# Split products with their input buffers at different distances into a kilobyte

## The chip, the cores and the metric

The kernel runs on one core of a Trainium2 chip. The core has a matrix engine (PE, TensorE), a vector engine (DVE, VectorE), an activation engine (ACT, ScalarE), GpSimd (POOL), a sync engine (SP) that here issues the transfers, an on-chip memory of 128 partitions that the engines read from, and an accumulation memory (`ps`, eight banks) that PE writes. The metric is the time of one execution on the device in microseconds, and lower is better.

## The reference, cut to what matters

Two transformer-like blocks are applied to 256 tokens of width 1024, in float32.

```python
# first block
h = rms_norm(x, norm1_g);  proj = h @ w_in            # 1024 x 11296
q, k, v, z, xbc, dt, g_attn, g_ssd = split(proj)
y_attn = moba_attention(norm(q), norm(k), v) @ w_attn_o
y_ssd  = ssd_mixer(z, xbc, dt, ...) @ w_ssd_o
x = x + (sigmoid(g_attn) * y_attn + sigmoid(g_ssd) * y_ssd) @ w_out
x = x + peer_ffn(rms_norm(x, norm2_g), w_peer_q, keys1, keys2, peer_u, peer_v)
# second block: two layers, each with a modulation from c @ ada_w
#   layer 0: neighbourhood attention and a gated recurrence, with 256 context tokens
#   layer 1: gated short convolution; after each a convolutional FFN of width 2816
# peer_ffn: per token and head, the 16 best of 128 x 128 expert pairs;
# act = x . peer_u[expert], out = sum(gelu(act) * gate * peer_v[expert])
```

Nearly all of the arithmetic is products of a weight matrix with the 256 tokens. The tables `peer_u` and `peer_v` have 16,384 rows of 1024, and the kernel multiplies with all of them and masks by the gates.

## The kernel before, in words

A float32 product is made of three matmuls in the type `fp32r`. Each operand is split into a high part and the remainder, and high x high, high x low and low x high are summed in the accumulation memory. This is `product` (lines 373 to 376):

```python
mm(o, w0, x0, ...)            # L374: weights high, input high
mm(o, w0, x1, ...)            # L375: weights high, input low
return mm(o, w1, x0, ...)     # L376: weights low, input high
```

The second argument of `mm` is the weights, a block of 128 x 128 that is loaded into the array (LDWEIGHTS, PEld in the profile). The third is the input, whose 256 columns stream through it. A slice of input is 256 float32, so 1024 bytes in each partition. `first_tiles` (lines 518, 519, 522) and the start of layer 0 (lines 852, 853, 856) write the same three matmuls in another order. In `rows` (lines 460 to 462) the roles are turned round: a block of the input is loaded as weights, and 512 columns of the weight matrix stream.

**The weights** come in units of 128 x 1024 float32 (4096 bytes in a partition). SP fetches each into one of seven slots of `raw`. ScalarE casts it into one of four slots of `wh`, the high part (L1109, `halves`), and VectorE subtracts, which leaves the low part in `wl` in the place of `raw` (L1560, `lows`); in part of the expert stage GpSimd does that (L2290). `wl` and `raw` are one area. PE frees the slots with its last matmul on a unit. A unit has eight blocks of 128 columns, and so 24 matmuls.

**The inputs** are pairs of buffers too. `xah`, `xal` (8 slices) hold the normalised input of most products. `xbh`, `xbl` (16 slices) hold what the output projections of the first block read. `hh` (4 slices) and `arenar0` to `arenar3` (32 slices each) hold the 128 blocks of activations of the experts. `xch`, `xcl` (8 slices) serve the context and the mixed heads in layer 0, `xfh`, `xfl` (22 slices) the FFNs. ScalarE writes the high part of a slice (L1145 and L1149 for `xah`), VectorE the remainder (L1598 and L1602 for `xal`). The rest of the work lies in big arenas `arena1`, `arenap`, `arena2` and `arena3`, cut into views.

**The order** of each engine's work is written out by hand, with semaphores between engines; nothing is planned at run time, and no order depends on an address. **The places** come from the allocator, which puts each tensor behind the last one that is still open on its stack. When a stack closes, the next tensor starts where that stack began. So the areas of the first block, of the expert stage and of the two layers lie over each other. Sizes that matter, in bytes per partition: `wl` 28672, `wh` 16384, `pcol` 2368, `cst` 1024, `modc` 768, `mab` 160, `small` 256, `xah` and `xal` 8192 each. Then come `J1` 2048, `sc1` 9216, `xbh` and `xbl` 16384 each, and `arena1` 99 x 1024.

Of the kernel before, what the change touches and what calls it, by code (L numbers as in the profile page):

```python
# [155 lines left out]
def build(nc, D, out):  # L156
    f32 = mybir.dt.float32
    f32r = mybir.dt.float32r
# [5 lines left out]
    es = ExitStack()  # L164
    with es:
        def sb(stack, name, shape, dt=f32):
            return stack.enter_context(nc.sbuf_tensor(name, shape, dt))
# [5 lines left out]
        m["wh"] = sb(es, "wh", [128, NSPLIT, 1024], f32r)  # L173
        pcol, cst = sb(es, "pcol", [128, NPC]), sb(es, "cst", [128, 2, 128])
        modc, mab, small = sb(es, "modc", [128, 2, 48, 2]), sb(es, "mab", [128, 5, 8]), sb(es, "small", [128, 64])
        xah, xal = sb(es, "xah", [128, 8, 256], f32r), sb(es, "xal", [128, 8, 256], f32r)
        with ExitStack() as part:
            J1, sc1 = sb(part, "J1", [128, 4, 128]), sb(part, "sc1", [128, 9 * 256])
            xbh, xbl = sb(part, "xbh", [128, 16, 256], f32r), sb(part, "xbl", [128, 16, 256], f32r)
            ar1 = sb(part, "arena1", [128, 99 * 256])  # L180
        with ExitStack() as part:
            with ExitStack() as plain_:
                arp = sb(plain_, "arenap", [128, 128 * 256])
            har = [sb(part, f"arenar{i}", [128, 32, 256], f32r) for i in range(4)]
            scp, hh = sb(part, "scp", [128, 8 * 256]), sb(part, "hh", [128, 4, 256], f32r)
        with ExitStack() as part:
            J2, sc2, x2t = sb(part, "J2", [128, 4, 128]), sb(part, "sc2", [128, 9 * 256]), sb(part, "x2", [128, 8, 256])
            with ExitStack() as layer:
                xch, xcl = sb(layer, "xch", [128, 8, 256], f32r), sb(layer, "xcl", [128, 8, 256], f32r)
                ar2 = sb(layer, "arena2", [128, 107 * 256])  # L190
            with ExitStack() as layer:
                xfh, xfl = sb(layer, "xfh", [128, 22, 256], f32r), sb(layer, "xfl", [128, 22, 256], f32r)
                ar3 = sb(layer, "arena3", [128, 64 * 256])
        spill = nc.dram_tensor("x_scratch", (128, 2048), f32, kind="Internal").ap().rearrange("p (a b) -> p a b", b=256)
        ps = [es.enter_context(nc.psum_tensor(f"ps{i}", [128, 512], f32)) for i in range(8)]
# [123 lines left out]
        STEPS, CTX, at = set(), 80, 2  # L319
# [2176 lines left out]
```

## Time and profile before

| | |
|---|---|
| median of 3 runs | 2088.43 us (2088.15 to 2090.45) |
| the profiled execution | 2089.99 us |
| its span, from the first to the last instruction | 2088.2 us, 40,173 instructions |
| matmuls | 16,718, PE busy 2037.9 us |
| VectorE, ScalarE, GpSimd busy | 1548.1, 1119.7 and 280.2 us |
| granted clock of PE, mean | 0.994 |

The duration of a matmul in the profile runs from its start to the modelled end of its last column. Matmuls overlap, so a duration (281 ns for most) is more than the time from one start to the next. The time that one costs is read from the starts, or from how many begin in a stretch.

### The profile page before, as it was taken

The numbers are of one execution on the slowest core, as the hardware profiler recorded it, in microseconds if no ns is written. First come the engines' busy times: TensorE is split into PE (matmuls) and PEld (weight loads), VectorE is DVE, ScalarE is ACT, GpSimd is POOL, SyncE is SP. The second block draws the span as 40 slices with busy tenths as digits, with TensorE's granted clock in tenths as the row PEclk, the third lists the DMA queues.
The fourth block names the chain that finished last, engine by engine and source line by source line (L and its number), as shares of the span: only waits on it lengthen the run. The fifth ranks groups of instructions, "written<-read, shape, count | busy, mean of one in ns | idle before, by whom it ended". The sixth has DMA issues, their size and how long they took to land.

```text
span 2088.2 us, 40173 instructions
## 1 busy us (share of the span) xinstructions
PE 2037.9 (98%) x16718; PEld 1984.0 (95%) x16718; DVE 1548.1 (74%) x2770; ACT 1119.7 (54%) x1742; POOL 280.2 (13%) x265
## 2 busy tenths in 40 slices
PE   7999999999999999999999999999999999999998
PEld 7898998999999999999999999998899998999998
DVE  6887789774999777877876667655567887867764
ACT  5567677545444666554544455555445554445553
POOL 0000000002887644420000000000110000000000
PEclk9999999999999999999999999999999999999999
DMA  5544433667555444446767777533115777655553
GB/s 194 166 152 137 153 121 112 219 205 248 188 184 188 134 142 142 142 152 215 255 236 237 265 244 252 172 108 111 50 54 196 246 250 261 216 186 172 184 181 121
DMA packets 104437, 375.43 MB, mean 180 GB/s; under 512 B 11584, under 2 KB 12224, under 8 KB 103872
## 3 DMA queue, kind: packets, MB, share of 16 engines
q1 hardware_dynamic: 104256, 372.86, 53.4%
q8 instruction: 133, 2.18, 0.4%
q14 instruction: 48, 0.39, 0.1%
HBM read 370.71 MB, written 2.10 MB: 179 GB/s over the span
## 4 chain that ended last, share of the span: by engine, by line
PE 73%; DVE 17%; ACT 5%; DMA 2%; issue 2%; POOL 0%; SPq 0%; POOLq 0%; DVEq 0%; ACTq 0%
PE ps L374 20%; PE ps L375 19%; PE ps L376 19%; DVE wl L1560 3%; PE ps L782 3%; DVE arenap L1918 2%; ACT wh L1109 2%; DVE arena L1713 1%; PE ps L571 1%; PE ps L460 1%; DVE arenap L1883 1%; PE ps L462 1%; PE ps L461 1%; DVE arenap L1878 1%; DMA raw<-in_ada 1%
## 5 line engine op out<-in xcount | busy, mean ns | idle before, releaser
L374 PE MATMUL ps<-xah,wh 128*128 128x256 f32 x2800 | 798.2, 285 | 7.0 <-DVE wl L1560 3.7
L375 PE MATMUL ps<-xal,wh 128*128 128x256 f32 x2800 | 787.0, 281 | 0.0
L376 PE MATMUL ps<-xah,wl 128*128 128x256 f32 x2800 | 786.6, 281 | 0.0
L1560 DVE TENSOR_TENSOR wl<-raw,wh 128x1024 fp32r<-128x1024 f32 (+2 forms) x539 | 637.7, 1204 | 186.5 <-ACT wh L1109 185.1
L1109 ACT ACTIVATE wh<-raw 128x1024 fp32r<-128x1024 f32 (+1 forms) x608 | 620.6, 1036 | 278.3 <-PE ps L376 135.0
L374 PEld LDWEIGHTS ps<-xah,wh 128*128 128x128 f32 x2800 | 527.9, 189 | 21.0 <-issue 9.0
L375 PEld LDWEIGHTS ps<-xal,wh 128*128 128x128 f32 x2800 | 528.2, 189 | 0.5 <-issue 0.2
L376 PEld LDWEIGHTS ps<-xah,wl 128*128 128x128 f32 x2800 | 528.0, 189 | 0.0
L2290 POOL TENSOR_TENSOR wl<-raw,wh 128x1024 fp32r<-128x1024 f32 (+1 forms) x69 | 162.8, 2365 | 1167.4 <-ACT wh L1109 1167.1
L374 PE MATMUL ps<-hh,wh 128*128 128x256 f32 x1024 | 289.9, 283 | 8.2 <-DVE wl L1560 6.5
L375 PE MATMUL ps<-arenar,wh 128*128 128x256 f32 x1024 | 287.7, 281 | 0.0
L376 PE MATMUL ps<-hh,wl 128*128 128x256 f32 x1024 | 287.7, 281 | 0.0
L374 PEld LDWEIGHTS ps<-hh,wh 128*128 128x128 f32 x1024 | 193.0, 188 | 9.6 <-DVE wl L1560 7.7
L375 PEld LDWEIGHTS ps<-arenar,wh 128*128 128x128 f32 x1024 | 193.0, 188 | 0.0
L376 PEld LDWEIGHTS ps<-hh,wl 128*128 128x128 f32 x1024 | 192.9, 188 | 0.0
L2297 POOL TENSOR_SCALAR hh<-cst,scp 128x128 fp32r<-128x128 f32 x192 | 117.3, 629 | 117.1 <-PE ps L782 117.1
L374 PE MATMUL ps<-xfh,wh 128*128 128x256 f32 x416 | 118.2, 284 | 2.4 <-DVE wl L1560 2.4
L376 PE MATMUL ps<-xfh,wl 128*128 128x256 f32 x416 | 117.6, 283 | 0.0
L375 PE MATMUL ps<-xfl,wh 128*128 128x256 f32 x416 | 117.5, 282 | 0.0
L1320 ACT ACTIVATE hh<-arenap 128x256 fp32r<-128x256 f32 x128 | 52.5, 412 | 115.2 <-PE ps L376 115.2
L1656 DVE SCALAR_TENSOR_TENSOR scp<-raw,small,scp 128x512 f32<-128x512 f32 x112 | 80.5, 749 | 28.0 <-DMA raw<-in_ada 26.6
L1958 DVE TENSOR_TENSOR arenar<-arenap,hh 128x256 fp32r<-128x256 f32 x128 | 53.3, 422 | 62.8 <-ACT hh L1320 62.2
(354 smaller groups left out, 3013.6 us busy)
## 6 DMA issues: line engine op xcount, KB each, us to landing
raw<-in_pu SPq DMA_DIRECT2D x128, 512.0 KB, 3.3
raw<-in_pv SPq DMA_DIRECT2D x128, 512.0 KB, 3.7
raw<-in_ada SPq DMA_DIRECT2D x96, 512.0 KB, 4.2
raw<-in_ff_up SPq DMA_DIRECT2D x88, 512.0 KB, 4.2
raw<-in_w_xbc SPq DMA_DIRECT2D x32, 512.0 KB, 3.3
raw<-in_ff_down SPq DMA_DIRECT2D x32, 512.0 KB, 4.0
raw<-in_w_z SPq DMA_DIRECT2D x16, 512.0 KB, 3.2
raw<-in_w_so SPq DMA_DIRECT2D x16, 512.0 KB, 4.2
```

Of the source, the lines that this page charges most:

```text
L374: mm(o, w0, x0, start=start, stop=False, skip_group_check=skip)
L375: mm(o, w0, x1, start=False, stop=False, skip_group_check=skip)
L376: return mm(o, w1, x0, start=False, stop=stop, skip_group_check=skip)
L782: last = mm(P[:, a * 128:a * 128 + 128], o[:, a, :].bitcast(f32), o2[:, a, :], start=True, stop=True)
L1109: put(W.hi(i), W.raw(i), ACT.Copy).then_inc(S["high"], 1)
L1320: put(hh[:, n % 4, :], HA[:, n, :], ACT.Copy).then_inc(S["h_hi"], 1)
L1560: tt_(W.lo(i), W.raw(i), W.hi(i).bitcast(f32), ALU.subtract).then_inc(S["lowV"], 1)
L1656: stt(dst, wv[:, kk, :], by, dst, ALU.mult, ALU.add).then_inc(step[0], 1)
L1918: last = stt(e4[:, :, :, j], p3, float(j), if16[:, tt, s, :, j:j + 1].to_broadcast([128, 8, 16]), ALU.is_equal, ALU.mult)
L1958: tt_(har[n // 32][:, n % 32, :], HA[:, n, :], hh[:, n % 4, :].bitcast(f32), ALU.subtract).then_inc(S["h_lo"], 1)
L2290: nc.gpsimd.tensor_tensor(W.lo(i), W.raw(i), W.hi(i).bitcast(f32), ALU.subtract).then_inc(S["lowG"], 1)
L2297: last = nc.gpsimd.tensor_scalar(ones1[g % 2][:, a, :], iota, lists[:, 0, 4 * g + a:4 * g + a + 1], None, ALU.is_equal)
```

## The change

In front of nine buffers a small tensor is allocated that nothing uses, just so long that the buffer begins at a chosen distance from a multiple of 1024 bytes. `begin` works out the pad from the distance at which the allocator stands, `last_end`, and that starts as 608. The streamed buffers then begin at 0 (`xah`), 64 (`xal`), 160 (`xbh`), 256 (`xbl`), 896 (`hh`), 480 (`xch`), 544 (`xcl`), 192 (`xfh`) and 352 (`xfl`). `arenar0` to `arenar3` follow from what is allocated before them. No instruction is added or removed.

```diff
-        xah, xal = sb(es, "xah", [128, 8, 256], f32r), sb(es, "xal", [128, 8, 256], f32r)
+        def begin(stack, name, at):
+            have = (last_end[0] + 31) // 32 * 32 % 1024
+            room = (at - have) % 1024
+            if room:
+                sb(stack, "before_" + name, [128, room // 4])
+            last_end[0] = at
+        last_end = [608]
+        begin(es, "xah", 0)
+        xah = sb(es, "xah", [128, 8, 256], f32r)
+        begin(es, "xal", 64)
+        xal = sb(es, "xal", [128, 8, 256], f32r)
         with ExitStack() as part:
             J1, sc1 = sb(part, "J1", [128, 4, 128]), sb(part, "sc1", [128, 9 * 256])
-            xbh, xbl = sb(part, "xbh", [128, 16, 256], f32r), sb(part, "xbl", [128, 16, 256], f32r)
+            begin(part, "xbh", 160)
+            xbh = sb(part, "xbh", [128, 16, 256], f32r)
+            begin(part, "xbl", 256)
+            xbl = sb(part, "xbl", [128, 16, 256], f32r)
+            last_end[0] = 64
             ar1 = sb(part, "arena1", [128, 99 * 256])
...
-            scp, hh = sb(part, "scp", [128, 8 * 256]), sb(part, "hh", [128, 4, 256], f32r)
+            scp = sb(part, "scp", [128, 8 * 256])
+            begin(part, "hh", 896)
+            hh = sb(part, "hh", [128, 4, 256], f32r)
+            last_end[0] = 64
...
-                xch, xcl = sb(layer, "xch", [128, 8, 256], f32r), sb(layer, "xcl", [128, 8, 256], f32r)
+                begin(layer, "xch", 480)
+                xch = sb(layer, "xch", [128, 8, 256], f32r)
+                begin(layer, "xcl", 544)
+                xcl = sb(layer, "xcl", [128, 8, 256], f32r)
+                last_end[0] = 64
...
-                xfh, xfl = sb(layer, "xfh", [128, 22, 256], f32r), sb(layer, "xfl", [128, 22, 256], f32r)
+                begin(layer, "xfh", 192)
+                xfh = sb(layer, "xfh", [128, 22, 256], f32r)
+                begin(layer, "xfl", 352)
+                xfl = sb(layer, "xfl", [128, 22, 256], f32r)
```

## Rows read from the trace of the kernel before

**Rows 1.** The page: busy time of the engines, and the chain that ended last.

```profile
PE 2037.9 (98%) x16718; PEld 1984.0 (95%) x16718; DVE 1548.1 (74%) x2770; ACT 1119.7 (54%) x1742; POOL 280.2 (13%) x265
...
PE 73%; DVE 17%; ACT 5%; DMA 2%; issue 2%; POOL 0%; SPq 0%; POOLq 0%; DVEq 0%; ACTq 0%
```

**Rows 2.** Busy time by windows: stretch, length, each engine's busy us (instructions), clock, DMA.

```profile
570.00:620.00 50.00, 50.00 (x425) 50.00 (x424) 47.86 (x144) 22.79 (x27) 43.35 (x18) 1.00 0.57 187
620.00:670.00 50.00, 50.00 (x425) 50.00 (x425) 49.79 (x53) 23.41 (x27) 42.12 (x18) 1.00 0.58 187
1000.00:1050.00 50.00, 50.00 (x426) 50.00 (x426) 38.87 (x56) 22.29 (x34) 0.00 (x0) 1.00 0.69 241
1980.00:2030.00 50.00, 50.00 (x425) 50.00 (x424) 34.06 (x49) 26.73 (x41) 0.00 (x0) 1.00 0.56 171
```

**Rows 3.** Timeline of PE, 600 to 603 us: start, duration, instruction.

```profile
600.18 0.28 PE L374 MATMUL ps<-xah,wh 128*128 128x256 f32 x1
600.30 0.28 PE L375 MATMUL ps<-xal,wh 128*128 128x256 f32 x1
600.41 0.28 PE L376 MATMUL ps<-xah,wl 128*128 128x256 f32 x1
600.53 0.28 PE L374 MATMUL ps<-xah,wh 128*128 128x256 f32 x1
...
600.89 0.28 PE L374 MATMUL ps<-xah,wh 128*128 128x256 f32 x1
...
603.02 0.28 PE L374 MATMUL ps<-xah,wh 128*128 128x256 f32 x1
```

**Rows 4.** Groups by line and form on PE: count, busy us, mean ns, idle before.

```profile
L374 PE MATMUL ps<-xah,wh 128*128 128x256 f32 x2800 | 798.2, 285 | 7.0 <-DVE wl L1560 3.7 <-POOL wl L2290 2.5 <-DVE xal L1843 0.7
...
L374 PE MATMUL ps<-hh,wh 128*128 128x256 f32 x1024 | 289.9, 283 | 8.2 <-DVE wl L1560 6.5 <-DVE arenap L1982 1.7
...
L374 PE MATMUL ps<-xfh,wh 128*128 128x256 f32 x416 | 118.2, 284 | 2.4 <-DVE wl L1560 2.4
...
L782 PE MATMUL ps<-scp,hh 128*128 128x128 f32 x512 | 62.5, 275 | 0.9 <-ACT hh L1305 0.9
L374 PE MATMUL ps<-xbh,wh 128*128 128x256 f32 x192 | 54.4, 283 | 0.7 <-DVE wl L1560 0.7
...
L374 PE MATMUL ps<-xch,wh 128*128 128x256 f32 x160 | 46.3, 289 | 0.6 <-POOL wl L2290 0.6
...
L518 PE MATMUL ps<-xah,wh 128*128 128x256 f32 x120 | 32.1, 295 | 0.4 <-ACT xah L1149 0.4
...
L852 PE MATMUL ps<-xah,wh 128*128 128x256 f32 x24 | 6.0, 281 | 0.0
```

**Rows 5.** Timeline of PE, 1402 to 1404 us.

```profile
1401.63 0.40 PE L460 MATMUL ps<-wh,xah 128*128 128x512 f32 x1
1401.87 0.39 PE L461 MATMUL ps<-wl,xah 128*128 128x512 f32 x1
...
1404.43 0.40 PE L460 MATMUL ps<-wh,xch 128*128 128x512 f32 x1
```

**Rows 6.** Timeline of PE, 905 to 908 us.

```profile
905.73 1.95 PE L782 MATMUL ps<-scp,hh 128*128 128x128 f32 x16
```

**Rows 7.** Instructions that write or read `xah`: count, shortest, median and longest in ns.

```profile
L1145 ACT ACTIVATE xah<-arena x16: 416/417/420, 18.3 to 462.8; 128x256 fp32r<-128x256 f32 x16
L1598 DVE TENSOR_TENSOR xal<-arena,xah x16: 418/422/426, 18.8 to 463.2; 128x256 fp32r<-128x256 f32 x16
```

## What the change was predicted to do

> **What bounds the kernel now.** I read the page first. The matrix engine (PE) is busy 98% of the span, and the chain that ended last lies on it for 73%, nearly all of that on lines 374 to 376, the three matmuls of a split product; VectorE holds 17% of the chain [rows 1]. "Busy" says little of a pipelined engine, so the next view was the one by windows, for the number of matmuls that start in a given time. In three far-apart stretches of 50 us there are 425, 425 and 426 of them [rows 2]: the engine starts them at a fixed beat, and that beat is the limit. The same rows show what the beat does not depend on. In the first, VectorE works 47.9 of 50 us and GpSimd 43.4; in the last, VectorE works 34.1 and GpSimd nothing, and the DMA share moves between 0.57 and 0.69; the clock is 1.00 in all of them, the 2.4 GHz level. Then the timeline gave the beat itself. From the matmul at 600.18 to the one at 603.02 there are 24 steps, so one takes 2.84/24 = 118.3 ns [rows 3]. 256 columns at 2.4 GHz are 106.7 ns; 11.7 ns of each step are something else.
>
> How much hangs on it: lines 374 to 376 run (2800 + 1024 + 416 + 192 + 160) x 3 = 13,776 times, lines 518, 519 and 522 together 360 times, and lines 852 and 853 48 times, with 24 more of line 856 that has the same form [rows 4]. That is 14,208 matmuls x 118.3 ns = 1681 us, 80% of the span. One nanosecond on each is 14.2 us, or 0.7%.
>
> **What the change is, in addresses.** It adds and removes no instruction, no wait and no transfer, and no order is changed. The pads are allocations that nobody writes or reads. Before, the `last_end = [608]` of the diff says where the first buffer began, and as every size up to `arena3` is a whole number of kilobytes, all ten split buffers, the J tables, the scratch and the arenas began at 608 bytes into a kilobyte. `wl` and `wh` lie in front: 28 + 16 kilobytes and 4576 bytes of columns and small tiles come after their start, so they began at 608 - 480 = 128, and they still do. After, the streamed operands begin at 0, 64, 160, 256, 480, 544, 192, 352 and 896, `arenar` at 64 like `xal`, and the arenas at 256, 64, 544 and 352. So the only thing that can move the time is a price that depends on the start address, in three places.
>
> **Place one: the streamed operand of 14,208 matmuls.** Does the 118.3 ns depend on where a stream of one kilobyte starts? Two things in the trace bear on it. First, the weights. Successive blocks of `wh` and `wl` are 512 bytes, so they start in turn at 128 and 640, while the streamed slices start at 608. A block takes three matmuls, 0.35 or 0.36 us in the rows, which round to 0.01 [rows 3]. A price for the distance between weights and stream, counted in a kilobyte, would make blocks alternate by more than that if it were above some 3 ns a matmul; it isn't. Second, the kernel has one kind of product with the roles turned round: lines 460 to 462 stream `wh` and `wl`, 512 columns at a start of 128, against weights from `xah`, `xal` and their like. From 1401.63 to 1404.43 there are 12 steps, 233.3 ns each [rows 5]. Two kilobytes at a start of 128 therefore cost 233.3, one at 608 costs 118.3; the second kilobyte costs 115.0 and a fixed part of 3.3 is left. With a fixed part of 3.3 ns per matmul the kilobyte has one price, 115.0 ns, at both starts. That fixed part isn't measured alone, and this gives the two bounds. If it were nothing, the kilobyte at 128 would cost 233.3/2 = 116.7 and that at 608 118.3, so 608 would be a poor place, and leaving it would be worth up to 1.6 x 14,208 = 24 us. If it were as large as that of a matmul of line 782, the kilobyte at 608 would be the cheap one. Sixteen of these take 1.95 us with the last's 0.275 in it, so (1.95 - 0.275)/15 = 111.7 ns a step, 5.0 above 106.7 [rows 4, 6]. The kilobyte would cost 113.3 at 608 and (233.3 - 5.0)/2 = 114.2 at 128, and leaving 608 would cost up to 0.85 x 14,208 = 12 us. I take 0: the two known starts agree within 1.6 ns under any fixed part in these bounds, and exactly at one well inside them.
>
> The Trainium skill has a rule that speaks against this change (SBUF — State Buffer, Specifications): the memory is read in 16-byte lines, and what costs is crossing to a new one. Old and new starts are all multiples of 32 bytes, so by it each kilobyte has 64 lines wherever it starts, and the sum is 0. No row here shows a start off such a line. It also has one that leaves room for a gain (TensorE: Matmul & The Clock Gate, Back-to-back issue gap): N/2.4 + 2.5 ns, 109.2 for 256 columns, with no word of addresses. The trace disagrees, 118.3 [rows 3]; were the whole difference due to the start, the sum would be an estimated 9.1 x 14,208 = 129 us of gain.
>
> **Place two: ScalarE and VectorE operations** that write or read the moved buffers. The cast to `xah` takes 416 to 420 ns over 16 slices and the remainder in `xal` 418 to 426 [rows 7]; their starts were all 608 and only these spreads are visible. VectorE has 17% of the chain, 355 us [rows 1]; 1% either way on it, as wide as that spread, is 3.6 us. It is a bound for both signs, and I take 0, as a group of operations has one duration over many addresses. ScalarE has 5% of the chain, so the same 1% there is 1 us. In most product stages these engines have room, so the cover is PE itself; it fails in 620 to 670, where VectorE works 49.79 of 50 us in the search for the largest scores [rows 2]. A slower VectorE would be seen there at once; a faster PE would be held up there.
>
> **Place three: transfers.** The DMA target `raw` is unmoved. The transfers into `xT`, J, `xc`, `x2` and `bias` go to moved tiles, but only a few of them and beside other work: 0.
>
> The sum is made against the profiled execution: 2089.99 us (its span is 2088.2), plus 0, is 2090.0. The median of the runs is 2088.43, 1.6 lower, and so is my figure: 2088.4.
>
> **The rivals.**
> *The stall of the streams is a matter of their start, and goes in part.* For it: 6.6 ns of each step are above what the line 782 matmuls need for the same weight load, and nothing in the trace accounts for them. Against it: two starts with the same price per kilobyte. If 608 is a poor place in the sense of the first bound, the gain is 24 us, 2064.7. A stronger form: only a stream that starts at 0 never crosses a kilobyte's edge, and `xah` is now such a one. It is streamed by lines 374, 376, 518, 519, 852 and 853, 5600 + 240 + 48 = 5888 times [rows 4]; down to 111.7 each saves 6.6 ns, 39 us in all, less what the VectorE-bound stretch keeps: 2050 at best.
> *The starts like 128 are the dear ones.* This is the other bound: 0, 64, 256, 192 and 896 are multiples of 64 like 128, while 608 is not. It decides if the fixed part is above 3.3 ns. The price is 0.85 ns a matmul, 12 us, if all the streams pay it: 2100.5. For it: the fixed part of line 782 is 5.0. Against: that figure can be the weight load's own and not the stream's.
> *A different start for the high and the low half costs at each change of stream.* In each three matmuls the stream goes from the high buffer to the low and back. Both began at 608; now they never do. If each change cost as little as 0.4 ns, 2/3 x 14,208 x 0.4 is 3.8 us, 2092.2; at 1 ns it is 9.5 us, 2097.9. No row shows such a change between unequal starts.
> *The change doesn't do what it says.* The pads are computed from the assumed 608; if another figure held, the buffers would be shifted together and the starts would still differ from each other by the same amounts. This changes no number above.
>
> **How the numbers follow.** A measurement of this kernel can tell 0.2%, 4.2 us, from no change. No change has 0.58. The stall going in part has 0.24: 0.15 for a gain of up to 24 us, 0.09 for more. Dear starts have 0.11 and the change of streams, in a size above 4.2 us, 0.07. So faster 0.24, same 0.58, slower 0.18. The range goes from 2070 to 2100: it holds the case of no change, most of the smaller gains (0.11) and most of the slower cases (0.14), 0.83 in all. The likeliest case alone would be 2085 to 2092.
>
> **What would show it.** In the profile after: between 422 and 428 matmuls in each of the stretches of 50 us, and 24 steps in 2.84 us for `xah`; 233.3 ns for the 512-column streams, whose start isn't moved, whatever happens to the rest. If the start matters, the beat will differ between buffers: `xah` with `xal` (0, 64), `hh` with `arenar` (896, 64), `xfh` with `xfl` (192, 352), `xch` with `xcl` (480, 544). One beat of 117.5 or less, or of 119.2 or more, on the first pair alone is enough to make the prediction wrong, as that pair has two thirds of the matmuls. A time that moves with the beat unmoved would mean place two: then the durations of the operations on moved tiles have changed.

## The result, and the profile after

The changed kernel takes 2094.7 us (median of 20 runs, 2088.4 to 2102.6) against 2089.4 us (20 runs, 2084.6 to 2096.0): a ratio of 1.0024, 95% interval 1.0013 to 1.0034. It is slower, by a quarter of a percent. Its runs cover 14.2 us, those of before 11.5 (standard deviations 4.0 and 2.6 us). One run of a kernel further down is left out of its ratio: 2475 us, with a granted clock of 0.75 where the others of that kernel have 0.99. The profiled execution was one of its fastest, 2088.84 us with a span of 2087.1. So the slowdown can't be read off its length; the beat of PE shows it.

First the page of after, the same two lines as in [rows 1].

```profile
PE 2039.2 (98%) x16718; PEld 1986.2 (95%) x16718; DVE 1550.8 (74%) x2770; ACT 1119.5 (54%) x1742; POOL 280.1 (13%) x265
...
PE 74%; DVE 17%; ACT 4%; DMA 2%; issue 2%; POOL 0%; SPq 0%; POOLq 0%; DVEq 0%; ACTq 0%
```

The busy shares moved by nothing that would tell of it. Now the windows of after: stretch, length, busy us (instructions) of PE, PEld, DVE, ACT, POOL, then clock and DMA. Four of them answer to [rows 2].

```profile
570.00:620.00 50.00, 50.00 (x416) 50.00 (x415) 47.82 (x145) 22.41 (x26) 41.48 (x18) 1.00 0.53 184
620.00:670.00 50.00, 50.00 (x416) 50.00 (x415) 49.79 (x49) 21.92 (x25) 42.78 (x18) 1.00 0.54 184
860.00:910.00 50.00, 50.00 (x433) 50.00 (x432) 41.54 (x85) 30.16 (x68) 22.90 (x39) 1.00 0.42 148
1000.00:1050.00 50.00, 50.00 (x428) 50.00 (x427) 39.64 (x57) 22.87 (x32) 0.00 (x0) 1.00 0.68 243
1980.00:2030.00 50.00, 50.00 (x427) 50.00 (x426) 34.08 (x49) 26.91 (x42) 0.00 (x0) 1.00 0.55 179
```

Read the number of matmuls in 50 us. It was 425 in both stretches of the experts' first half; it is 416. It was 426 and is 428 on `hh` and `arenar`, and 425 and 427 in the last FFN. PE is 100% busy each time and the clock is 1.00, so only the count tells. The three matmuls of a product (a step of 355.0 ns before, three times the 118.3 of [rows 3]) now have two beats on `xah` and `xal`. The timeline of after shows both; every third start is a new product:

```profile
640.08 0.28 PE L400 MATMUL ps<-xah,wh 128*128 128x256 f32 x1
...
640.45 0.28 PE L400 MATMUL ps<-xah,wh 128*128 128x256 f32 x1
...
641.53 0.28 PE L400 MATMUL ps<-xah,wh 128*128 128x256 f32 x1
...
1985.07 0.28 PE L400 MATMUL ps<-xah,wh 128*128 128x256 f32 x1
...
1986.13 0.28 PE L400 MATMUL ps<-xah,wh 128*128 128x256 f32 x1
```

Four products take 641.53 - 640.08 = 1.45 us (363 ns each) at 640, and three take 1.06 us (353) at 1985. Taken over all starts of the trace, the pairs behave so, in ns per product:

| pair and starts | before | after |
|---|---|---|
| `xah` 0, `xal` 64 | 355.0 | 353.3, or 363.3, now and then 360.0 |
| `hh` 896, `arenar` 64 | 355.0 | 353.3 |
| `xbh` 160, `xbl` 256 | 355.0 | 353.3 |
| `xfh` 192, `xfl` 352 | 355.0 | 353.3 |
| `xch` 480, `xcl` 544 | 355.0 | 353 to 354 in long stretches, 355 to 357 where eight products stand alone |

In this trace a beat holds from one interruption to the next (a wait of PE, or matmuls of another form), whether that is 14 steps or 454. The two operations shown in [rows 7] kept their durations: the cast to `xah` 417 to 420 ns, the remainder 412 to 425. One part of VectorE's work did get longer, the search for the largest scores; it comes up under the sum below.

### The profile page after: what moved, and what is told of

It is laid out like the page before. It is cut to its first block, busy times and chain, and to the rows that moved or that the text cites. A ratio compares the mean times of both kernels' runs of the same rounds, so it can differ in the third digit from the quotient of the medians.

```text
span 2087.1 us, 40173 instructions
## 1 busy us (share of the span) xinstructions
PE 2039.2 (98%) x16718; PEld 1986.2 (95%) x16718; DVE 1550.8 (74%) x2770; ACT 1119.5 (54%) x1742; POOL 280.1 (13%) x265
## 3 DMA queue, kind: packets, MB, share of 16 engines
q8 instruction: 133, 2.18, 0.4%
## 4 chain that ended last, share of the span: by engine, by line
PE 74%; DVE 17%; ACT 4%; DMA 2%; issue 2%; POOL 0%; SPq 0%; POOLq 0%; DVEq 0%; ACTq 0%
PE ps L400 20%; PE ps L401 20%; PE ps L402 19%; DVE wl L1586 3%; PE ps L808 3%; DVE arenap L1944 2%; ACT wh L1135 1%; DVE arena L1739 1%; DMA raw<-in_ada 1%; PE ps L597 1%; PE ps L486 1%; DVE arenap L1909 1%; PE ps L488 1%; PE ps L487 1%; DVE arenap L1904 1%
## 5 line engine op out<-in xcount | busy, mean ns | idle before, releaser
L1135 ACT ACTIVATE wh<-raw 128x1024 fp32r<-128x1024 f32 (+1 forms) x608 | 620.2, 1036 | 286.1 <-PE ps L402 136.5
```

The source lines that it names most:

```text
L1135: put(W.hi(i), W.raw(i), ACT.Copy).then_inc(S["high"], 1)
```

## The experiments

**Which buffers.** The first two kernels take the change apart.

```diff
 # only_xa: xah at 0, xal at 64, everything else back at 608
+        begin(es, "all", 608)
-            begin(part, "xbh", 160)
+            begin(part, "xbh", 608)      # and so for xbl, hh, xch, xcl, xfh, xfl
 # not_xa: the reverse
-        begin(es, "xah", 0)
+        begin(es, "xah", 608)            # and xal at 608, all others as in the change
```

> Only xah (0) and xal (64) are moved; all other streamed buffers and the arenas stay at 608. Theory (start of the streams): the product of three matmuls on xah and xal takes either 353.3 ns or 363.3 ns, and which one is settled anew after each pause; on all other pairs it takes 355.0 as before. So the slowdown of the change stays and its small gain on the other pairs goes: 1.003 to 1.006 of before. Rival (the arenas and the scratch moved, and VectorE or ScalarE pay): 1.000, and 355.0 everywhere. Rival (the whole shift is noise between programs): within 0.1% of before, with the two beats hidden behind other waits.

Measured: 1.0036 (1.0024 to 1.0048), 2096.0 us. The trace has 355 on the other pairs. On `xah` and `xal`, counted in stretches of six or more, some 1,350 products take 353, 180 take 360 or 361 and 1,020 take 363.

> The reverse: xah and xal stay at 608, and all other pairs and the arenas begin where the change puts them. Theory: 355.0 ns a product on xah and xal, 353.3 on the 1792 products of the other pairs, so 3 us less than before, 0.9985, and little spread between runs. Rival (the arenas and VectorE pay): slower than before by about 0.2%, as the change.

Measured: 0.9991 (0.9982 to 1.0001), 2087.4 us, with 355 on `xah` and `xal` and 353 on nearly all the rest. The interval doesn't tell the 3 us from nothing, but it excludes the slowdown. So the loss comes with one pair, and the new places of the arenas have no visible part in it.

> The change with xah at 896 in place of 0 (xal stays at 64): the pair of starts that hh and arenar have in the change, where every product took 353.3 ns. Theory: 353.3 on all 4736 products, so (4736 x 1.67) 7.9 us less than before, 0.996, with little spread. Rival (it is the number of products or the work beside them on xah and xal that brings the long beat, and not where they start): the long beat of 363.3 stays in the same stages, 1.002.

```diff
-        begin(es, "xah", 0)
+        begin(es, "xah", 896)
```

Measured: 0.9982 (0.9972 to 0.9992), 2086.2 us. The long beat is gone: about 2,500 products on the pair at 352 to 354. It is the starts and not the work beside them. The gain is half of what I expected; the last experiment shows where the rest goes. Little spread, which I had expected twice, didn't come either: the runs cover 12.1 us here and 8.4 with `xah` and `xal` at 608.

**The same program twice.**

> The changed kernel once more, for a second profile. Theory (each stretch of products takes its beat at its start, and not always the same in two executions): another set of stretches on xah and xal shows 363.3, all other pairs again 353.3 throughout, and a product more on the long beat is worth up to 10 ns of span against the first profile. Rival (the program fixes the beats): the same stretches as in the first profile show 363.3, and the span stays within 1 us of 2087.1.

Measured: 2099.07 us, span 2097.3, 10.2 us more than the first profile of the same program. These are the windows of this second execution:

```profile
620.00:670.00 50.00, 50.00 (x415) 50.00 (x414) 49.79 (x49) 22.44 (x26) 42.74 (x18) 1.00 0.51 180
860.00:910.00 50.00, 50.00 (x423) 50.00 (x422) 41.60 (x88) 29.43 (x65) 23.70 (x41) 1.00 0.39 136
1000.00:1050.00 50.00, 50.00 (x428) 50.00 (x427) 39.95 (x58) 24.99 (x35) 0.00 (x0) 1.00 0.72 253
1980.00:2030.00 50.00, 50.00 (x416) 50.00 (x415) 34.84 (x54) 27.30 (x45) 0.00 (x0) 1.00 0.53 175
```

The stretches 860 to 910 and 1980 to 2030 changed from 433 to 423 and from 427 to 416, with 1000 to 1050 the same. Of some 2,550 products of the pair in stretches of six or more, about 945 had the long beat in the first execution and 1,665 in the second: 720 x 10 ns is 7.2 us, and 110 more at 360 make it 8. A stretch at the 1.2 GHz level that only the second trace has (at 1126 us) accounts for another 1.7. The program doesn't fix the beat. That adds to the spread of the changed kernel's runs but isn't all of it: the runs of before cover 11.5 us, and its trace has one beat throughout. The granted clock varies too, from 0.991 to 0.995 in runs of before.

**What the beat depends on.** A program of its own runs only products on one pair of weight buffers and one of streams, at chosen starts, with pauses between:

```python
W0, W1 = (t[:, s // 4 + 128 * q:s // 4 + 128 * q + 128] for t, s in ((wh, w), (wl, u)))
X0, X1 = xh[:, h // 4 + 256 * k:h // 4 + 256 * k + 256], xl[:, l // 4 + 256 * k:l // 4 + 256 * k + 256]
mm(o, W0, X0, ...)
mm(o, W0, X1, ...)
last = mm(o, W1, X0, ...)
```

> A program of its own, which leaves the whole computation out: the three matmuls of a product, sixteen products in a row, after pauses of six kinds, for 28 sets of starts of weights, high stream and low stream. No other engine works beside it but for short ScalarE casts in the pauses. Theory A (the distance between stream and weights, counted in a kilobyte, sets the beat): weights 0 with streams 480 and weights 544 with streams 0 behave as weights 128 with streams 608, 355.0 ns. Theory B (the start of the stream alone): weights 0 or 544 make no difference to streams 0 and 64, which show 353.3 or 363.3. Theory C (the distance between high and low stream): all sets with equal starts give 355.0, and those 64 apart the two beats. If only the work of VectorE and GpSimd beside PE brings the long beat, no set here shows it.

Measured, in ns per product (the times of different pauses, from the starts in the timeline):

| weights | streams high, low | ns | streams minus weights |
|---|---|---|---|
| 128 | 608, 608 | 355 | 480 |
| 0 | 480, 480 | 355 | 480 |
| 544 | 0, 0 | 355 | -544 |
| 32 | 512, 512 | 355 | 480 |
| 128 | 96, 96 | 355 | -32 |
| 128 | 0, 64 | 353, 360 or 363 | -128, -64 |
| 0 | 896, 960 | 353, 360 or 363 | 896, 960 |
| 544 | 416, 480 | 353 or 363 | -128, -64 |
| 128 | 128, 128; 0 and 0, 0 alike | 360 | 0 |
| 128 | 0, 0 | 356 or 360 | -128 |
| 128 | 64, 64 | 340 or 353 | -64 |
| 128 | 160, 160 | 350, once 353 | 32 |

Theory A is right and stronger than I had it: 480, -544 and -32 are the same number modulo 256, and so are -128 and 896. Theory B falls on 0, 0: 360 with weights at 0 and 356 or 360 with weights at 128. Theory C falls on 64, 64, which has two beats with equal starts. No other engine worked beside PE here, so what PE does itself is enough for the effect. That its two reads meet in the memory, the weights for the next matmul and the stream of this one, is the natural reading; no run shows what happens inside.

> The program of its own again, with the whole computation left out: all sets start the weights at 128. First sixteen sets with both streams at the same distance, 0 to 240 bytes in steps of 16, then the 56 sets with two different distances in steps of 32. Theory (each matmul's time depends on the distance of its stream from the weights that are loaded beside it, modulo 256 bytes): the distance 192 (which is 64 in front) gives 353.3 and 340.0 as start 64 did, 224 gives 355.0, 0 gives 360.0, 32 gives 350.0; and a set with distances c and d lies between what c and d give alone. Rival (the period is a kilobyte): the distance 192 behaves otherwise than 64 in front.

Measured, with both streams at one distance, for 0, 16, 32, ... 240 bytes: 360, 350 or 356, 350 (353 once), 355, 353, 355 or 360, 360, **340**, 356 or 360, 356, 352 or 356, 358, **340 or 353**, 350 or 358, 355, 352. The period of 256 holds. With two different distances the sum isn't a mean of the two: all 56 sets lie at 349 to 360 and none is as good as the equal pair at 112. (The fourth program has one set of 112 with 192; it took 347 after some pauses and 356 to 361 after others.)

> The program of its own, with the whole computation left out, for what settles the beat: five sets of starts, fifty stretches each of twelve products, after ten kinds of pause in turn (one to five small float32 matmuls, or a wait for ScalarE of five lengths). Theory A (the kind of pause fixes it): at starts 0 and 64 every fifth of the same kind shows the same beat. Theory B (it is where the pause ends against a slower clock): the same kind shows both. Starts 608 show 355.0 and starts 240 show 340.0 after every kind.

Measured at starts 0 and 64: after two or four of the small matmuls always 353, after one, three or five always 363, after waits for ScalarE both. (The very first stretch was still at the slower clock.) In the timeline of that program, six products after two and six after three small matmuls:

```profile
21.20 0.28 PE L48 MATMUL ps<-xh,wh 128*128 128x256 f32 x1
...
23.32 0.28 PE L48 MATMUL ps<-xh,wh 128*128 128x256 f32 x1
...
26.13 0.28 PE L48 MATMUL ps<-xh,wh 128*128 128x256 f32 x1
...
28.31 0.28 PE L48 MATMUL ps<-xh,wh 128*128 128x256 f32 x1
```

2.12 us against 2.18. So at these starts A holds for pauses of PE's own, and those that another engine ends give both beats; that the reason is the moment at which such a pause ends, as B has it, is not shown. The kind isn't all, though: in the first survey, at the same starts, two small matmuls gave 363 and four gave 360. With both streams at 64 the kind alone decides in this program: 353 after two or four small matmuls, 340 after all others, waits included. Streams at 608 show 355 after every kind. Those at 240 show 340 in the end after every kind, but after some kinds the first two to four products of a stretch take 345 to 358 before it settles.

**Into the kernel.**

> All ten streamed buffers and the arenas begin at 64, so 64 bytes before the weights, the distance at which the survey showed 353.3 ns a product after some pauses and 340.0 after others. Theory (the distance of each stream from the weights sets the beat, and the start of a stretch which of two it is): every product of the kernel shows 353.3 or 340.0, never 360 or more; 4736 products x 1.67 = 8 us less than before if all take the long one, 4736 x 15 = 71 us if all take the short one; 2018 to 2082. Rival (the survey's 340.0 needs idle engines beside PE, or equal content): 353.3 throughout, 2082. Rival (different starts of high and low are what helped hh, xb, xc and xf): 355.0, no change.

```diff
-        begin(es, "xah", 0)
+        begin(es, "xah", 64)             # and all other streamed buffers at 64
```

Measured: 0.9926 (0.9899 to 0.9952), 2072.4 us, 2061.6 to 2079.0. Both beats appear on every pair, 340 to 344 on some 2,040 products and 353 on 2,155, none longer. The theory stands; the rivals don't.

> The same with all at 160, 32 bytes behind the weights, where the survey showed 350.0 ns after nearly all pauses. Theory: 350.0 to 353.3, so 4736 x 5 = 24 us less at best, 2066 to 2082. Rival (only the survey, without other engines, shows it): 355.0, no change.

Measured: 0.9936 (0.9916 to 0.9956), 2076.8 us. Of the products in longer stretches some 3,665 take 350 and 530 take 353 or 354.

> The weights begin 16 bytes later in their slots (144 modulo 256) and all streams at 256, so each stream begins 112 bytes behind the weights modulo 256, the distance at which the second survey showed 340.0 ns a product after every pause. Theory (distance alone): 340.0 on all 4736 products, in every stage; that is 15.0 ns less on each, 71 us if PE is the limit everywhere, and some 10 us of it kept by VectorE where it works 49.8 of 50 us: 2018 to 2032, with a small spread. Rival (with other engines at work the good distance is not stable): two beats again, 2050 to 2075. Rival (a start off 32 bytes costs on VectorE and ScalarE): PE at 340.0 and the time above 2040.

```diff
-        m["wl"] = sb(es, "wl", [128, NRAW, 1024], f32r)
+        m["wl"] = off(sb(es, "wl", [128, NRAW * 1024 + 64], f32r), NRAW)   # starts 16 bytes in
```

Measured: 1.0047 (1.0034 to 1.0061), 2100.2 us: a miss, and slower than anything. The products took 350, 355 or 360. VectorE and ScalarE kept their durations (1204 and 1035 ns for the two splits of a unit, 1204 and 1036 before), so neither rival named the reason. Only 630 or so products came down to 350, and 2,300 took 358 to 361.

> The program of its own, with the whole computation left out, twenty sets of starts in which high and low weights are set apart. Question: why distance 112 gave 350 to 360 in the kernel. If weights off a multiple of 32 are the reason, the set 144, 144, 256, 256 shows 350 or more, and 160, 160, 272, 272 and 0, 0, 112, 112 show 340. If it is that high and low weights were 256 apart (400 and 144), the set 400, 144, 256, 256 alone is long, and 128, 384, 240, 240 too. If neither, both show 340 and the cause is elsewhere in the kernel. Starts 496, 752 and 1008 for the streams show what 240 shows if the period is 256 bytes.

Measured: weights 144 with streams 256 give 360 after every pause. Weights 160 with 272, 128 with 240, 0 with 112 and 256 with 368 settle at 340, after up to four products at 345 to 357. All have a distance of 112. Six products each, at weights 144 and at weights 128:

```profile
34.00 0.28 PE L51 MATMUL ps<-xh,wh 128*128 128x256 f32 x1
...
36.16 0.28 PE L51 MATMUL ps<-xh,wh 128*128 128x256 f32 x1
...
206.77 0.28 PE L51 MATMUL ps<-xh,wh 128*128 128x256 f32 x1
...
208.81 0.28 PE L51 MATMUL ps<-xh,wh 128*128 128x256 f32 x1
```

High and low weights 256 apart changed nothing (128, 384 with 240: 340), nor did streams at 496, 752 or 1008. So a distance keeps the beat that it settles at when both starts move by a multiple of 32 bytes, in all sets tried, but not when they move by 16. That cuts both ways: weights 144 with streams 624 (distance 224) take 360 where 128 with 608 take 355, but weights 144 with streams 80 (distance 192) settled at 340 after every kind of pause, where 128 with 64 has two beats. This explains the products at 360 in the kernel with all at 112. Where its 350 and 355 come from stays open: the program of its own shows only 360 at those starts.

> The weights stay at 128. All streams but hh and arenar begin at 240 modulo 256, so at the very starts that gave 340 to 343 ns in both surveys; hh and arenar begin at 64 as in the run with all at 64. Theory (the distance counts, and starts that are an odd multiple of 16 must be on the side of the stream as in the survey): 340 on all 3712 products of the other pairs, 340 or 353.3 on the 1024 of hh and arenar; 3712 x 15 + 1024 x 1.7 = 57 us less at most, 10 us of it kept by VectorE: 2031 to 2045. Rival (the kernel's weights lie in seven and four slots of 4 kilobytes and the survey's in one, and that is why 112 failed): 350 to 360 again, 2085 to 2102.

```diff
+        def stream(stack, name, n, at):
+            begin(stack, name, at)
+            last_end[0] = at + 32
+            return sb(stack, name, [128, n * 256 + 8], f32r)[:, 4:4 + n * 256].rearrange("p (a b) -> p a b", b=256)
-        xah = sb(es, "xah", [128, 8, 256], f32r)
+        xah = stream(es, "xah", 8, 736)  # begins at 752, 240 modulo 256; xal, xb, xc, xf too
```

Measured: 0.9861 (0.9841 to 0.9882), 2059.8 us, the best of all: 30 us less than before and 35 less than the change. The products settle at 340 on all pairs but `hh` and `arenar`, which show 340 or 353. Many short stretches begin with two or three products at 353, as in the survey, and so average 343. The rival on slots falls. A window of before and four of this kernel, and PE's wait in its view of waits:

```profile
660.00:680.00 20.00, 17.53 (x148) 17.32 (x148) 15.87 (x27) 9.98 (x13) 11.45 (x6) 1.00 0.59 185
...
570.00:620.00 50.00, 50.00 (x443) 50.00 (x443) 47.97 (x139) 23.98 (x28) 45.41 (x20) 1.00 0.59 198
620.00:670.00 50.00, 44.05 (x389) 43.85 (x387) 49.28 (x63) 19.50 (x23) 33.78 (x14) 0.97 0.55 182
660.00:680.00 20.00, 11.01 (x81) 10.81 (x80) 11.91 (x31) 6.95 (x9) 8.45 (x6) 0.74 0.28 94
1920.00:1970.00 50.00, 50.00 (x444) 50.00 (x443) 37.79 (x56) 29.03 (x46) 0.00 (x0) 1.00 0.58 196
...
PE ps L398 <- POOL wl L2314: 9.0, 1, 9.0
```

443 and 444 matmuls in 50 us, where there were 425. The gain was less than the 45 to 57 us forecast. Summed over the steps of the trace, the shorter beats are worth 50 us; the span is 32.5 us shorter. About half of the difference goes in the stretch in the middle. VectorE works 49.28 of 50 us, PE gets ahead of it and then waits, once, for 9.0 us (2.5 in the kernel before); its clock fell to 1.2 GHz for 10.2 us. Against the kernel before, the same matmul came 11.6 us earlier at 660 and 4.7 us earlier at 680. The rest goes in smaller pieces elsewhere; the whole trace has 42.9 us at the 1.2 GHz level, the one of before 27.5. `xah` at 896 lost its gain in the same place: 2.6 us ahead before the stretch, 2.1 behind after it, with 6.8 us at 1.2 GHz. (That is the trace of its slowest run, 2090.2 us; its median is 2086.2.)

## Why the prediction was wrong

**The step that failed** is place one, "I take 0". PE's beat does depend on where a stream starts: on the first pair it went from 118.3 ns a matmul to 117.8 or 121.1, past the 119.2 that I had named as a sign of being wrong. It depends on the distance from the weights modulo 256, and I had two arguments against that, both blind to it. The measured time, 2094.7 us, lies inside the range from 2070 to 2100 all the same, but that is luck: none of the causes that the range was drawn for brought it there.
- *Successive weight blocks at 128 and 640 would alternate, were there a price for the distance.* They are 512 bytes apart, two whole periods. An even beat excluded a period of a kilobyte, not one of 256 bytes.
- *Two starts, 608 and 128, have one price per kilobyte.* With the roles turned the distance is 128 - 608 = -480, so 32 modulo 256; in the products it is 224. The comparison was of two distances that are close in price (350 and 355 a product in the surveys) and said nothing of the other fourteen. My bounds, 0.85 to 1.6 ns a matmul, were bounds for those two starts. The measured span over all distances is 340 to 363 a product, so 5 ns a matmul to the good and 2.8 to the bad.

**The sum with the measured beats.** The first execution of the change has, against 355.0, about 1,550 products of the pair at -1.7 ns, 950 at +8.3 and 70 at +5, and 1,792 of the other pairs at -1.7: +2.7 us. The second has +10.6. Measured in the spans are -1.1 and +9.1. Two more things lie between. One is the slow clock: the trace of before has 27.5 us at the 1.2 GHz level, these two have 23.5 and 24.7, which at half speed is worth 2.0 and 1.4 us. The other is the long stretch of 455 products from 513 to 679. It costs PE 3.8 us in both sums, but the chain lies on VectorE there, and PE waits at its end anyway. What counts is how long VectorE's search takes, from its cast to its last reduction (start and duration, before and then after; the times in ns are shortest, median and longest):

```profile
L1896 DVE CAST arenap<-arenap x1: 1168/1168/1168, 565.5 to 565.5; 128x512 f32<-128x512 uint32 x1
L1922 DVE TENSOR_REDUCE arenap<-arenap x4: 2286/2286/2290, 630.0 to 672.3; 128x128 f32<-128x2048 f32 x4
...
L1922 DVE CAST arenap<-arenap x1: 2297/2297/2297, 564.5 to 564.5; 128x512 f32<-128x512 uint32 x1
L1948 DVE TENSOR_REDUCE arenap<-arenap x4: 2285/2286/2287, 631.2 to 674.4; 128x128 f32<-128x2048 f32 x4
```

That is 109.1 us before and 112.3 after, with the same operations: 3.2 us more, and they are VectorE's. The times are 112.2 in the second execution and in only_xa, which have the 363 beat in this stretch too, and 109.0 in not_xa. So they go with `xah` and `xal` and not with the new places of the arenas. The operations that got longer ran while GpSimd worked: of the 16 additions in L1899, the eight with no GpSimd operation beside them take 404 to 415 ns in all these traces, and the eight with one take 651 to 707 in before and not_xa and 718 to 831 in the other three. Why they fall differently beside GpSimd is not shown; other kernels here have 108.5 to 111.8. With these terms the sums are +0.1 and +8.6 us, against -1.1 and +9.1. The median of 20 runs lies between, at +5.3.

**The rivals.** Dear starts had the right sign and 11%, but another mechanism: it made all multiples of 64 dear, and `hh`, `arenar` and `xfh` at such starts became quicker. A price for each change between high and low doesn't exist as such (160 and 256 are quicker than two equal starts at 608). The stall going in part was right for four of the five pairs: 1.7 ns a product. The pair with nearly two thirds of the products went the other way in part of its stretches.

**What stood.** Place three. Place two stood for the casts and remainders of the streams, and not_xa has the moved arenas without a loss, but it had missed that VectorE's search can change its length, by 3.2 us, with no address of its own involved. The figure of 0.7% per nanosecond is an upper bound: in the last kernel 5 ns on about three quarters of the matmuls would be 56 us, of which it kept 30. The note that a faster PE would be held up at 620 to 670 came true. The sentence on 512-column streams was wrong: their start didn't move, but the start of their weights (`xah`, `xch`) did, and their mean step fell from 233.2 to 232.3 ns (231 to 233 by stretch, where all were 233).

**The Trainium skill's rules.** The runs show starts that are all multiples of 32 at 340, 350, 353, 355 and 363 ns, so the number of 16-byte lines, by which I would have had 0 (Trainium skill, SBUF — State Buffer, Specifications), isn't what decides. The Trainium skill says too that PE has two independent read ports and that loading the next weights "doesn't steal SBUF read bandwidth from the running matmul" (TensorE: Matmul & The Clock Gate, Step-by-step: what each phase is for). The surveys speak against that for this type and size: with nothing beside PE, the same stream takes 113 to 121 ns a matmul as the distance to the weights varies.

## What to carry to other kernels

Count the matmuls that start in 50 us in a stretch with PE 100% busy. If the step is well above the 113.3 ns that the best distance gave here (256 columns of `fp32r`), the distance between weights and stream may be what costs, and a survey program of one to two milliseconds finds a good one. Spreading the starts is not the remedy, for a stream can land on a distance with two beats; put all of them at the one distance that settles at the short beat after every kind of pause. Use the very starts that the survey tried, or move both by a multiple of 32 bytes: moved by 16, the good distance of 112 was lost. Then look at the next engine in line: a third of what PE won here (50 us by its beats, 32.5 in the span) was lost to waits and the slower clock. And an agreement between two addresses excludes a dependence only for periods that tell them apart.

## What the runs showed that I had not expected

- A stretch of back-to-back matmuls keeps its beat, for as long as 455 products (165 us); at the starts that settle at 340 the first products, up to four, can be longer. Which beat it takes depends on the pause before it, within one program down to the number of small matmuls in it, and at some starts on the execution where another engine ends the pause.
- 340.0 ns a product is 113.3 a matmul; 363.3 is 121.1. The 128-column matmuls of line 782, 111.7 ns a step by [rows 6] and 111.3 to 111.6 by their own starts, kept that in every kernel, whatever the starts.
- A matmul stream that got faster made PE wait at the next stage that VectorE limits, long enough for the clock to fall to 1.2 GHz. Before there was no such fall there.
- The same VectorE operations took 109 or 112 us for the search, depending on how GpSimd's fell beside them. A loss of 3 us in another engine can look like the beat's.
- Open: why two beats exist, what 16 bytes change for the weights, and why the search changes its length. None was taken further.
